# The FFN up stage of a two-layer encoder step, rewritten with seven block products per hidden tile

## What is computed

```python
def half_ffn(x, g, w_gu, w_down):
    gate, up = jnp.split(rmsnorm(x, g) @ w_gu, 2, axis=-1)
    return x + FFN_RESIDUAL * ((jax.nn.silu(gate) * up) @ w_down)
```

## Time and profile before

| what | us |
|---|---|
| median of 3 runs (2206.19 to 2213.73) | 2212.01 |
| the profiled execution's own time | 2216.53 |
| its span, first to last instruction | 2214.4 |
| TensorE busy, 16810 matmuls | 2155.9 (97%) |
| VectorE busy | 1055.3 (48%) |
| ScalarE busy | 658.5 (30%) |
| GpSimd busy | 283.2 (13%) |
| weight stream, 323 chunks of 512 KB | 3.4 each from issue to landing |

### The profile page before, as it was taken

One profiled execution on the slowest core, in us unless ns is written; L12 is line 12 of the kernel. 1 busy time (PEld: TensorE's weight loads), 2 busy tenths in 40 slices (PEclk: granted clock), 3 DMA queues, 4 the chain that ended last, 5 costly groups with the idle time before them and its releaser, 6 DMA issues.

```text
span 2214.4 us, 42345 instructions
## 1 busy us (share of the span) xinstructions
PE 2155.9 (97%) x16810; PEld 2066.1 (93%) x16810; DVE 1055.3 (48%) x1519; ACT 658.5 (30%) x997; POOL 283.2 (13%) x281
## 2 busy tenths in 40 slices
PE   7999999999999999999999999999999999999996
PEld 7999999997679999999999999999966799999996
DVE  7444433353755544443344444333456574444334
ACT  4222222224643322222232232222245432222222
POOL 2000001212334000001100000122043230000012
PEclk9999999999999999999999999999999999999998
DMA  4222222431001222222222222325310022222222
GB/s 150 87 89 89 86 96 95 167 126 54 11 21 58 95 85 85 93 88 96 95 78 87 92 85 86 96 94 188 105 35 11 30 70 93 85 89 90 93 98 79
DMA packets 54663, 191.05 MB, mean 86 GB/s; under 512 B 6360, under 2 KB 8280, under 8 KB 54040
## 3 DMA queue, kind: packets, MB, share of 16 engines
q1 hardware_dynamic: 47664, 171.59, 23.7%
q10 hardware_dynamic: 6900, 18.10, 2.2%
HBM read 182.85 MB, written 7.41 MB: 86 GB/s over the span
## 4 chain that ended last, share of the span: by engine, by line
PE 79%; issue 13%; POOL 3%; DVE 2%; DMA 1%; ACT 1%; ACTq 0%; DVEq 0%; POOLq 0%; SPq 0%
PE banks L933 74%; POOL probs L674 1%; PE banks L1062 1%; DVE xg_lo L698 1%; DMA raw<-w_stream 1%; PE banks L1166 1%; POOL uq_lo L678 1%; PE banks L1130 1%; PE banks L1098 1%; PE banks L1049 0%; POOL sq L640 0%; ACT w_hi L421 0%; PE banks L952 0%; DVE w_lo L694 0%; POOL zq_lo L669 0%
## 5 line engine op out<-in xcount | busy, mean ns | idle before, releaser
L933 PE MATMUL banks<-xg_hi,w_hi 128*128 128x272 f32 x3456 | 725.7, 291 | 19.3 <-DVE xg_lo L698 19.2
L933 PE MATMUL banks<-xg_lo,w_hi 128*128 128x272 f32 x3456 | 716.5, 288 | 0.0
L933 PE MATMUL banks<-xg_hi,w_lo 128*128 128x272 f32 x3456 | 716.0, 288 | 0.0
L933 PEld LDWEIGHTS banks<-xg_hi,w_hi 128*128 128x128 f32 x3456 | 542.8, 189 | 23.6 <-DVE xg_lo L698 21.9
L694 DVE SCALAR_TENSOR_TENSOR w_lo<-raw,w_hi 128x1024 fp32r<-128x1024 f32 (+1 forms) x323 | 423.9, 1312 | 295.3 <-ACT w_hi L421 294.5
L933 PEld LDWEIGHTS banks<-xg_lo,w_hi 128*128 128x128 f32 x3456 | 547.8, 189 | 0.0
L933 PEld LDWEIGHTS banks<-xg_hi,w_lo 128*128 128x128 f32 x3456 | 542.5, 188 | 0.0
L421 ACT ACTIVATE w_hi<-raw 128x1024 fp32r<-128x1024 f32 (+1 forms) x323 | 333.0, 1033 | 623.5 <-PE banks L933 578.7
L933 PE MATMUL banks<-h_hi,w_hi 128*128 128x272 f32 x1408 | 292.2, 289 | 0.0
L933 PE MATMUL banks<-h_lo,w_hi 128*128 128x272 f32 x1408 | 290.3, 287 | 0.0
L933 PE MATMUL banks<-h_hi,w_lo 128*128 128x272 f32 x1408 | 290.0, 287 | 0.0
(11 more groups left out here) (126 smaller groups left out, 1591.5 us busy)
## 6 DMA issues: line engine op xcount, KB each, us to landing
raw<-w_stream SPq DMA_DIRECT2D x323, 512.0 KB, 3.4
mla_quv<-w_mla ACTq DMA_DIRECT2D x2, 2048.0 KB, 10.4
bias<-bias_in ACTq DMA_DIRECT2D x2, 1698.5 KB, 6.7
x<-x_in SPq DMA_DIRECT2D x4, 272.0 KB, 6.2
x<-x_in ACTq DMA_DIRECT2D x4, 272.0 KB, 6.3
av_out<-vt ACTq DMA_DIRECT2D x2, 544.0 KB, 2.8
ak_out<-ak ACTq DMA_DIRECT2D x2, 544.0 KB, 4.0
ckv_out<-ckv ACTq DMA_DIRECT2D x2, 544.0 KB, 3.2
```

The costliest lines, as they stand in the source:

```text
L933: done = mm(banks[:, 2 * (job % PAIRS) + half, 0:HALF], w[slot][:, wk], v[:, half * HALF:(half + 1) * HALF], start=first and n == 0, stop= ...
```

## The change

**Products.** The hidden tile's 256 x 544 result (gate and up features by two halves of 272 tokens) is a 2 x 2 block product: weights A11, A12 (gate, rows 0 to 3 and 4 to 7 of x's tiles), A21, A22 (up, the same), tokens B11, B12 / B21, B22. It is made with seven block products in Winograd's form, each 4 row tiles x 3 terms = 12 matmuls of 272 columns: p1 = A11 B11, p2 = A12 B21, p3 = S4 B22, p4 = A22 T4, p5 = S1 T1, p6 = S2 T2, p7 = S3 T3. The weight sums are S1 = A21+A22, S2 = S1-A11, S3 = A11-A21, S4 = A12-S2; the token sums T1 to T4 of x are made once per FFN. TensorE adds what it can in PSUM: p6 on p1 (then ScalarE copies u2), p7 on that, p4 on that, p3 on p5. The four quarters are read as c11 = p2 + s1 (a copy of p1), c12 = (p5+p3) + u2, c22 = (p1+p6+p7) + p5, and c21 directly, times the gate.

**Who does what in one tile's cycle.** GpSimd: four weight sums (128 x 512 each) for the tile after next, and the gate's first product with rstd (544 columns). ScalarE: seven high parts of 512 columns, copies of s1, p5, u2 out of PSUM (272), silu, and h_hi, which was VectorE's. VectorE: seven low parts of 512 columns, c11, c12, c22, the gate's second product with rstd, both halves of the hidden tile, h_lo. Units S1, A11, A12, S4 have one place each in SBUF, S2, S3, A22 two.

**Two phases.** Each FFN runs 11 hidden tiles up, then a down stage over these 11 for all 8 output tiles (chunks of 8 and 3 tiles, x updated after each), then the other 11: 4 phases per layer in place of 2. There are four `raw` buffers instead of two, and 176 chunks per layer instead of 160. The input and output projections use a ring of three units instead of four, made two ahead. The order of row and output tiles is 0, 4, 1, 5, 2, 6, 3, 7. In the first phase of an FFN the norm's root and reciprocal are made between the fifth product and the first tile's cycle. The token sums (ScalarE b and high parts, VectorE sums and low parts) are made beside the last output tiles of the stage before; at the kernel's start, after all of xg. They stand also in the last down stage of the kernel.

Cut to what the text below speaks of:

```diff
-RAW, SPLIT, PAIRS, LEAD = 2, 4, 4, 3
+PHASES = 2
+PAIR_N = NH // PHASES
+DOWN_TILES = (8, PAIR_N - 8)
+RAW, PAIRS, LEAD = 4, 4, 2
+RING = 3
...
+DOWN_ORDER = [(0, 0), (1, 0), (0, 1), (1, 1)] + [(j, part) for j in range(2, KD) for part in range(2)]
...
+def slots_of(unit):
+
+    if unit[0] == "up":
+        n, role = unit[2:]
+        return ({"A11": 0, "S1": 1, "A12": 2, "S4": 3, "S2": 4 + n % 2, "S3": 6 + n % 2, "A22": 8 + n % 2}[role],)
...
+            for c in range(2, RAW):
+                sp.dma_start(raw[c][:, :], w_stream[c]).then_inc(raw_loaded[c], 16)
+            later_chunks = w_stream[RAW:STREAM].rearrange("(l c) p w -> l c p w", c=CHUNKS)
+            with sp.Fori(0, DEPTH) as l:
+                for c in range(CHUNKS):
+                    sp.wait_ge(lo_split, nth(lo_split, l, LAST_OF[c] + 1))
+                    sp.dma_start(raw[c % RAW][:, :], later_chunks[l, c]).then_inc(raw_loaded[c % RAW], 16)
...
+            def up_cycle(l, p, n, i=0, tile=None):
+
+                more = n + 2 < PAIR_N
+                copy_s1(l, p, n + 1, i)
+                make_hi(l, ("up", p, n + 1, "S4"), i)
+                make_hi(l, ("up", p, n + 1, "S3"), i)
+                silu(l, p, n, i)
+                copy_p5(l, p, n + 1, i)
+                make_hi(l, ("up", p, n + 2, "A11") if more else ("down", p, 0), i)
+                make_hi(l, ("up", p, n + 1, "A22"), i)
+                hidden_hi(l, p, n, i, n if tile is None else tile)
+                make_hi(l, ("up", p, n + 2, "A12") if more else ("down", p, 1), i)
+                if more:
+                    make_hi(l, ("up", p, n + 2, "S1"), i)
+                copy_u2(l, p, n + 1, i)
+                if more:
+                    make_hi(l, ("up", p, n + 2, "S2"), i)
+
...
+            def weight_sum(l, p, n, role, i=0, lap=0):
+
+                unit = ("up", p, n, role)
+                total = weights(unit)[2]
+                a11, a12, a21, a22 = (raw_of(("up", p, n, a)) for a in ("A11", "A12", "A21", "A22"))
+                gate_c, up_c = (chunk_of(("up", p, n, a))[0] for a in ("A11", "A22"))
+                for c in (gate_c, up_c):
+                    pool.wait_ge(raw_loaded[c % RAW], l * (16 * CHUNKS // RAW) + (i * 16 + (lap * (16 * CHUNKS // RAW) + (c // RAW + 1) * 16)))
+                pool.wait_ge(chunk_used, nth(chunk_used, l, i * LOOP_UNITS + (lap * UNITS + FREED[unit])))
+                if role in ("S2", "S4"):
+                    pool.wait_ge(sums_made, nth(sums_made, l, i * 8 + (lap * PL[sums_made] + sum_count(p, n, role) - 1)))
+                if role == "S1":
+                    done = nc.gpsimd.tensor_tensor(total, a21, a22, ALU.add)
+                elif role == "S2":
+                    done = nc.gpsimd.tensor_tensor(total, weights(("up", p, n, "S1"))[2], a11, ALU.subtract)
+                elif role == "S4":
+                    done = nc.gpsimd.tensor_tensor(total, a12, weights(("up", p, n, "S2"))[2], ALU.subtract)
+                else:
+                    done = nc.gpsimd.tensor_tensor(total, a11, a21, ALU.subtract)
+                done.then_inc(sums_made, 1)
+
+            def scale_gate(l, p, n, i):
+                count = i * 2 + (pair_index(p, n) + 1)
+                pool.wait_ge(c12_read, nth(c12_read, l, count))
+                nc.gpsimd.tensor_tensor(gate[:, :], gate[:, :], rstd[:, :], ALU.mult).then_inc(gate_scaled, 1)
+
+            def up_cycle(l, p, n, i=0):
+
+                scale_gate(l, p, n, i)
+                if n + 2 < PAIR_N:
+                    for role in SUMS:
+                        weight_sum(l, p, n + 2, role, i)
+
...
+            def token_sums(l, which, j, lap=0):
+
+                kk = j // 2
+                count, bs = t_count(which, kk) + lap * KD, KD * (which - 1) + j + 1 + lap * 2 * KD
+                dve.wait_ge(b_set, nth(b_set, l, bs))
+                lower, upper = slice(0, HALF), slice(HALF, T)
+                if j % 2 == 0:
+                    nc.vector.tensor_tensor(t_sum[:, 0, kk, :], gate[:, upper], gate[:, lower], ALU.subtract).then_inc(t1_made, 1)
+                    return
+                nc.vector.tensor_tensor(t_sum[:, 2, kk, :], up[:, upper], gate[:, upper], ALU.subtract).then_inc(t3_made, 1)
+                dve.wait_ge(t3_made, nth(t3_made, l, count))
+                nc.vector.tensor_tensor(t_sum[:, 1, kk, :], t_sum[:, 2, kk, :], gate[:, lower], ALU.add).then_inc(t2_made, 1)
+                dve.wait_ge(t2_made, nth(t2_made, l, count))
+                nc.vector.tensor_tensor(t_sum[:, 3, kk, :], up[:, lower], t_sum[:, 1, kk, :], ALU.subtract).then_inc(t4_made, 1)
...
+            def finish_gate(l, p, n, i):
+                count = i * 2 + (pair_index(p, n) + 1)
+                dve.wait_ge(gate_silu, nth(gate_silu, l, count))
+                nc.vector.scalar_tensor_tensor(gate[:, :], gate[:, :], 1.0, rstd[:, :], ALU.mult, ALU.mult).then_inc(gate_ready, 1)
+
+            def make_hidden(l, p, n, i):
+
+                g = pair_index(p, n)
+                dve.wait_ge(chunk_used, nth(chunk_used, l, i * LOOP_UNITS + (USED_AT[("up", p, n, "A22")] + 1)))
+                dve.wait_ge(gate_ready, nth(gate_ready, l, i * 2 + (g + 1)))
+                nc.vector.tensor_tensor(up[:, 0:HALF], banks[:, X_OF[n % 2], 0:HALF], gate[:, 0:HALF], ALU.mult).then_inc(c21_read, 1)
+                dve.wait_ge(c22_read, nth(c22_read, l, i * 2 + (g + 1)))
+                nc.vector.tensor_tensor(up[:, HALF:T], up[:, HALF:T], gate[:, HALF:T], ALU.mult).then_inc(h_made, 1)
+
...
+            def up_cycle(l, p, n, i=0, tile=None):
+
+                more = n + 2 < PAIR_N
+                read_c12(l, p, n, i)
+                if n + 1 < PAIR_N:
+                    make_lo(l, ("up", p, n + 1, "S2"), i)
+                    make_lo(l, ("up", p, n + 1, "S4"), i)
+                else:
+                    make_lo(l, ("down", p, 2))
+                read_c22(l, p, n, i)
+                if n + 1 < PAIR_N:
+                    make_lo(l, ("up", p, n + 1, "S3"), i)
+                    make_lo(l, ("up", p, n + 2, "A11") if more else ("down", p, 0), i)
+                else:
+                    make_lo(l, ("down", p, 3))
+                finish_gate(l, p, n, i)
+                make_hidden(l, p, n, i)
+                if n + 1 < PAIR_N:
+                    make_lo(l, ("up", p, n + 1, "A22"), i)
+                    read_c11(l, p, n + 1, i)
+                hidden_lo(l, p, n, i, n if tile is None else tile)
+                if n + 1 < PAIR_N:
+                    make_lo(l, ("up", p, n + 2, "A12") if more else ("down", p, 1), i)
+                if more:
+                    make_lo(l, ("up", p, n + 2, "S1"), i)
+
+            def down(l, p):
...
+            def product(l, p, n, role, bank, hi, lo, fresh, i=0, ready=None):
+
+                unit = ("up", p, n, role)
+                made(l, unit, i)
+                unit_hi, unit_lo, _ = weights(unit)
+                for k in range(KD // 2):
+                    if ready is not None:
+                        pe.wait_ge(ready[0], nth(ready[0], l, ready[1](k)))
+                    wk = slice(k * P, (k + 1) * P)
+                    for step, (w, v) in enumerate(((unit_hi, hi), (unit_hi, lo), (unit_lo, hi))):
+                        done = mm(banks[:, bank, 0:HALF], w[:, wk], v[k], start=fresh and k == 0 and step == 0,
+                                  stop=k == KD // 2 - 1 and step == 2, skip_group_check=True)
+                done.then_inc(chunk_used, 1)
+
...
+            def up_begin(l, p):
+
+                which, phase = divmod(p, PHASES)
+                ready = [None] * 4
+                if phase == 0:
+                    norm = N_UP2 if which else N_UP1
+                    ready = [(xg_set, lambda k: tile_count(norm, k)), (t1_set, lambda k: t_count(which, k)),
+                             (xg_set, lambda k: tile_count(norm, KD // 2 + k)), (t_set, lambda k: t_count(which, k))]
+                pe.wait_ge(result_read, nth(result_read, l, phase_job(p, 0) - 1))
+                p1(l, p, 0, ready=ready[0])
+                p5(l, p, 0, ready=ready[1])
+                pe.wait_ge(result_read, nth(result_read, l, phase_job(p, 0)))
+                p2(l, p, 0, ready=ready[2])
+                p3(l, p, 0)
+                if phase == 0:
+                    if which == 0:
+                        pe.wait_ge(const_loaded, 16)
+                    pe.wait_ge(sq_sum, nth(sq_sum, l, norm * KD))
+                    sum_of(sqacc, SUM_PAIR).then_inc(norm_summed, 1)
+                p6(l, p, 0, ready=ready[3])
+
+            def up_cycle(l, p, n, i=0):
+                p1(l, p, n + 1, i)
+                p7(l, p, n, i)
+                p5(l, p, n + 1, i)
+                p4(l, p, n, i)
+                p2(l, p, n + 1, i)
+                p3(l, p, n + 1, i)
+                p6(l, p, n + 1, i)
```

(44 more changed lines are left out.)

760 lines of the change are left out of this document (518 added, 242 removed).

## The result

The changed kernel takes 2341.57 us (median of 4 runs, 2339.5 to 2342.45); the kernel before took 2212.21 beside it (4 runs). The ratio is 1.0589, 95% interval 1.0568 to 1.061: slower by 129 us. The prediction said slower, 2275, between 2205 and 2345. The direction and the range held. The size did not: +129 instead of +63.

A forecast was written before the change was run, and what follows sets the result against it. VectorE, held by GpSimd on operands in SBUF, was to bound the up stage: cycle 12.2 us. Up stages of 1153 us against 1093.5 give +59.5, the kernel's end about +3: 2275 against the median, range 2205 to 2345.

The forecast's parts named there:

- The steady tile: Up stage, one hidden tile's cycle: 12.2 us against 12.05 before, 7.4 of VectorE's own work and 4.75 held by GpSimd.
- Rival 1: Up stage: TensorE stays the bound, GpSimd's sums fall into VectorE's idle time; cycle 10.54, kernel 2135 us; chance 0.13.
- rival 3: Up stage: no PSUM reads hidden, or waits add up; cycle 12.9 to 13.2, kernel 2325 to 2350 us; chance 0.20.
- The w_lo with a mean of 0.9 us or more: Up stage sign: VectorE's 512-column low part averages 0.9 us or more, where alone it would be 0.69.
- The first down product: Sign for the first phase: the first matmul product of the down stage starts near 180 us.
- One TensorE gap per tile: Up stage sign: TensorE stands still about 1.6 us per tile before p4, until VectorE's c22 read.
- the start after the output projection: Two phase starts: VectorE and GpSimd want about 5 us per tile against 3.0 given; 8 us more, 28 each.
- The projections' ring at nothing: Projections: rings of three units have a 6 us job as cover, so they were counted as costing nothing.
- The other starts and the tail: Starts: 60 us at kernel start, 20 after the earlier layer's down stage, 10.3 for each inner phase; kernel end about +3.
- forecast case: Whole kernel, the likeliest outcome: cycle 11.9 to 12.5 us, time 2240 to 2325 us; chance 0.50.
- Rival 2: Most PSUM reads hidden, starts 0 to 20 us shorter; cycle 11.5 to 11.8, kernel 2195 to 2240 us; chance 0.15.
- The clock: TensorE's clock falls after idle gaps; at 1.2 GHz throughout, cycle 19 us and kernel above 2700; chance 0.02.

## Why the prediction was right in direction and short by half

**The steady tile: right.** The prediction said that an op with two SBUF inputs on VectorE or GpSimd stands still while the other engine has one, from the earlier trace rows, and walked a tile to 12.2 us. The tile measured 12.38 in the same order, against 12.05 before; the cut sums (10.51, 10.95), the moved gate product (11.89) and the moved sums (10.79) each went where this puts them. Rival 1 (TensorE stays the bound) and rival 3 (cycle 12.9 and more, nothing hidden) are out: two of four PSUM reads did lie beside GpSimd's ops. The 19 ops alone, those of 512 columns 0.60 to 0.62 us apart at 0.68 to 0.69 each, show the next one starting some 0.08 us before the last one's end. The Trainium skill ("VectorE: DVE Perf Modes", section "The DRAIN you can't avoid") says that the next op does not start until the pipe empties, and, at the end of the same paragraph, that a next op that is not held starts earlier. The trace agrees with the second. The prediction took up the first alone, so its 0.07 us per op and the 12.8 us of its third rival were not what the page gives for these ops.

**The other signs.** The w_lo with a mean of 0.9 us or more: measured 1.69 for those made from raw data and 1.07 for those made from w_sum. The first down product, forecast near 180, started at 185.6. GpSimd's time per tile was given as "over 6.4"; it is 8.1, since it is held as well. One TensorE gap per tile, ended by c22: 1.4 us where 1.6 was said.

**The step that failed: the start after the output projection.** The prediction gave "its jobs give 3.0 us per tile while VectorE and GpSimd want about 5 there together: 8 us more, 28". VectorE took 6.35 us per tile (720.1 to 770.9 for eight), and the start 42.6. This is 29 of the 63 us. The sum was wrong in itself: 2 us more per tile over eight tiles are 16, not 8. At the measured 6.35 the same sum gives 27; the start was 22.6 over the 20 that it was added to. "About 5" was a guess too; the stage was never walked as the cycle was. Walked, it has per pair two x updates, two or three low parts, four token sums and their two low parts, all in one queue, with a ScalarE part in front of four of them. The runs split the excess: 7 to 8 us per layer are holds by the squares, 3.3 the round trips, and with both gone 30.6 are left, against 28.

**The cycle term was undersized**, by 0.2 us in 12.2: nine cycles in eight phases are 72 x 0.2 = 14.4 of the 19.9 us that the phases are longer. The other 5.5 lie in the last tile of each phase: a down stage's 528 matmuls take 66.0 us (185.6 to 253.1, less p4's 12 matmuls that stand among them) where 66.3 was forecast. What in the last tile takes this 1 us more stays open.

**The projections' ring at nothing: wrong.** The cover named was a 6 us job. It was not enough for ScalarE, which issues nine loads for 5 to 5.6 us of it; 2.3 to 2.5 us per layer came of it, and in the run that moved the chunk ahead they are gone. One thing stays open: the second layer's projections and attention were 0.6 us shorter than before in spite of that gap.

**The other starts and the tail.** After the layer's down stage 26.6 against 20, the tail +7.1 against +3. In both, token sums stand between the last x updates. Moving the starts' weight sums to VectorE cut the first by 3.6 us and the tail by 4.7 (29.2 to 24.5), so part of both was their holds; the rest stays open. The kernel's start lost 9.1 in the same run, but there the token sums moved too, and no run separated the two.

**The range held by luck.** The time is 3.4 us under its upper edge. The range gave the starts 20 us, and they missed by 37.5 (2.1, 29.2, 6.6, less 0.4), with 4.1 more in the tail; the room that was meant for the cycle, 50 us, took this up. The total lies in what rival 3 was given (2325 to 2350), though its cycle of 12.9 is refuted, and outside the forecast case of 2240 to 2325. Rival 2's lower end, 2195, does not come out of its own terms either: cycle 11.5 and 20 us off the starts give 2205.

**The clock: small in the cycle, not in the starts.** See the last section.

## What to carry to other kernels

If one engine's ops hold another's, add their times as if they were one engine, and leave out only what reads PSUM: in this kernel 14 ops on VectorE and 5 on GpSimd took 12.4 us, and all 19 on VectorE alone 10.8. Work that is moved to an idle engine is not free because that engine is idle. And walk each kind of stage start with its queue order, not only the steady cycle: four terms that were summed from guesses carried more of the miss than the loop that runs 72 times.
